# Splitting the last differential-attention head by component and moving modulation units by one tile

## What is computed

```python
sc = einsum('bqhcd,bkhcd->bhcqk', qb, k) * scale      # c: two components of 64
p = softmax(sc, axis=-1)
p = p[:, :, 0] - lam * p[:, :, 1]
o = einsum('bhqk,bkhd->bqhd', p, v)                   # v of 128 columns per head
o = rmsnorm(o, subln_g) * (1 - lambda_init)
y = (o * silu(z)) @ w_out0
```

## Time and profile before

| | us |
|---|---|
| median of 3 runs | 2986.59 |
| lowest, highest | 2982.62, 2989.71 |
| the profiled execution | 2981.39 |
| its span | 2979.5 |
| PE busy in it | 2772.0 (93%) |
| PEld busy | 2167.8 (73%) |
| DVE busy | 1681.5 (56%) |
| ACT busy | 1318.2 (44%) |

### The profile page before, as it was taken

How to read it: one execution, slowest core, us unless ns; L and a number is a source line. 1 busy time by engine, 2 the same in 40 slices (tenths; PEclk the granted TensorE clock), 3 DMA queues, 4 the chain that set the end, 5 groups by cost and what they waited for, 6 DMA issues and landing times.

```text
span 2979.5 us, 35047 instructions
## 1 busy us (share of the span) xinstructions
PE 2772.0 (93%) x13125; PEld 2167.8 (73%) x13125; DVE 1681.5 (56%) x2233; ACT 1318.2 (44%) x1881; POOL 0.2 (0%) x4
## 2 busy tenths in 40 slices
PE   6999999996899989999998899988799999999998
PEld 4777777774677767777776667666577878878787
DVE  7678888887676534344455635554764434434345
ACT  5666676664324134444343435655434323223233
POOL 0000000000000000000000000000000000000000
PEclk9999999997899999999999899999799999999999
DMA  7311111101443300000012210000211111111112
GB/s 255 104 35 50 44 34 49 49 28 56 163 134 124 113 16 16 9 6 9 6 42 98 72 40 22 22 15 15 99 36 49 44 48 48 45 49 41 52 40 84
DMA packets 216227, 168.36 MB, mean 57 GB/s; under 512 B 9578, under 2 KB 203074, under 8 KB 216130
## 3 DMA queue, kind: packets, MB, share of 16 engines
q1 hardware_dynamic: 215648, 166.88, 17.9%
q10 hardware_dynamic: 482, 0.18, 0.0%
HBM read 153.92 MB, written 13.11 MB: 56 GB/s over the span
## 4 chain that ended last, share of the span: by engine, by line
PE 79%; DVE 8%; ACT 6%; DMA 2%; DVEq 2%; issue 2%; SPq 0%; ACTq 0%
PE PS L510 18%; PE PS L512 17%; PE PS L511 17%; PE PS L1295 4%; PE PS L1957 4%; PE PS L1268 2%; PE PS L1282 2%; PE PS L1923 2%; PE PS L1272 1%; PE PS L1947 1%; PE PS L2442 1%; PE PS L2455 1%; DMA gated<-in_w_ada 1%; PE PS L2466 1%; PE PS L1915 1%
## 5 line engine op out<-in xcount | busy, mean ns | idle before, releaser
L510 PE MATMUL PS<-h_high,w_high 128*128 128x512 f32 x2096 | 845.8, 404 | 46.7 <-DVE w_low L532 18.4
L511 PE MATMUL PS<-h_low,w_high 128*128 128x512 f32 x2096 | 826.0, 394 | 0.0
L512 PE MATMUL PS<-h_high,w_low 128*128 128x512 f32 x2096 | 825.9, 394 | 0.0
L510 PEld LDWEIGHTS PS<-h_high,w_high 128*128 128x128 f32 x2096 | 399.7, 191 | 148.0 <-issue 42.5
L512 PEld LDWEIGHTS PS<-h_high,w_low 128*128 128x128 f32 x2096 | 399.0, 190 | 86.2
L511 PEld LDWEIGHTS PS<-h_low,w_high 128*128 128x128 f32 x2096 | 399.9, 191 | 80.1 <-issue 1.5
L532 DVE TENSOR_TENSOR w_low<-raw_weights,w_high 128x1024 fp32r<-128x1024 f32 (+2 forms) x156 | 179.4, 1153 | 160.3 <-ACT w_high L527 159.4
L527 ACT ACTIVATE w_high<-raw_weights 128x1024 fp32r<-128x1024 f32 (+2 forms) x156 | 155.9, 1000 | 233.7 <-PE PS L512 232.0
L1372 ACT ACTIVATE residual<-PS,rest 128x1024 f32<-128x1024 f32 x128 | 141.4, 1110 | 178.9 <-DVE rest L1502 178.9
L2998 DVE SCALAR_TENSOR_TENSOR gated<-rest,gated 128x1024 f32<-128x1024 f32 x44 | 56.6, 1286 | 254.2 <-ACT gated L2966 254.2
L849 DVE SCALAR_TENSOR_TENSOR residual<-PS,rest,residual 128x512 f32 (+1 forms) x104 | 76.4, 749 | 157.8 <-PE PS L512 153.6
(11 more groups left out here) (338 smaller groups left out, 4073.5 us busy)
## 6 DMA issues: line engine op xcount, KB each, us to landing
raw_weights<-in_w_in SPq DMA_DIRECT2D x59, 512.0 KB, 4.1
raw_weights<-in_w_up SPq DMA_DIRECT2D x44, 512.0 KB, 3.8
gated<-in_w_ada SPq DMA_DIRECT2D x12, 1536.0 KB, 7.1
raw_weights<-in_w_out SPq DMA_DIRECT2D x24, 512.0 KB, 5.0
rest<-in_ada_w SPq DMA_DIRECT2D x16, 576.0 KB, 4.9
activations<-in_ada_w SPq DMA_DIRECT2D x8, 1024.0 KB, 14.0
x_kept<-residual SPq DMA_DIRECT2D x2, 4096.0 KB, 12.5
residual<-x_kept SPq DMA_DIRECT2D x2, 4096.0 KB, 12.9
```

The lines of the kernel that those rows point to most:

```text
L510: e.matmul(out_, wh[:, k, :], xh[:, k, cols], start=first, stop=False)
L511: e.matmul(out_, wh[:, k, :], xl[:, k, cols], start=False, stop=False)
L512: return e.matmul(out_, wl[:, k, :], xh[:, k, cols], start=False, stop=last_k)
```

## The change

The last head gets its own procedures. Scores, maximum and exponential are done for each component by itself, the transposes of a block come two rounds after its scores, and the gate's products move from rounds 1 to 4 to rounds 3 to 6. The output projection has `early=7`: its first two weight tiles are split inside the head and on its end, G's first seven tiles get their high and low parts there, and TensorE multiplies them before the eighth is there. `gate_b` moves from the place of the high parts to that of the low parts. Unit 0's load waits for the last head's V transposes instead of the gating, and its products stand before the last gating. In the projection, unit u's products and matmuls come one tile later; unit 6 goes to the input projection of layer 1 with buffer `MIX_C`. Cut to its core:

```diff
-    gate_b = view(h_at, NT, HALF)
+    gate_b = view(h_at + NT * S, NT, HALF)
-    mix_stage = [view(at, NT, MCH) for at in (sc_at + 2 * S, g_at, g_at + 5 * S)]
+    mix_stage = [view(at, NT, MCH) for at in (sc_at, g_at, g_at + 5 * S)]
...
@@ OutProj.sync
             if self.units:
-                for sm, v in self.src_ready:
-                    wait(e, sm, v)
+                e.wait_ge(*self.first_unit_free)
                 mix_load(e, 0, MIX_A)
                 e.wait_ge(self.gl, self.bg + self.kt)
                 mix_load(e, 1, MIX_B)
-            with e.Fori(0, 3) as it:
+            with e.Fori(0, 2 if self.units else 3) as it:
                 for j in range(2):
                     e.wait_ge(s["ws_low"], 2 * it + (self.tile + j + 1))
                     e.dma_start(self.raw(j), self.w[:, :, bass.ds(2 * P * it + (2 + j) * P, P)]).then_inc(self.full[j], 16)
                     if self.units:
                         e.wait_ge(s["md_acc"], 2 * it + (MIX_M + 1 + j))
                         mix_load(e, 2 * it + (2 + j), (MIX_A, MIX_B)[j])
+            if self.units:
+                for j in range(2):
+                    e.wait_ge(s["ws_low"], self.tile + j + 5)
+                    e.dma_start(self.raw(j), self.w[:, :, (6 + j) * P:(7 + j) * P]).then_inc(self.full[j], 16)
+                mix_load(e, 6, MIX_C)
+                e.wait_ge(s["md_acc"], MIX_M + 6)
+                mix_load(e, 7, MIX_B)
@@ OutProj.tensor
-            if self.b == 1:
+            if self.b < 2:
                 self.rest_pe(e)
+                self.unit_pe(e, 0)
...
                 for j in range(2):
                     self.tile_pe(e, 2 * it + j, j)
-                    self.unit_pe(e, 2 * it + j)
+                    self.unit_pe(e, 2 * it + (j - 1))
             self.tile_pe(e, 6, 0)
-            self.unit_pe(e, 6)
+            self.unit_pe(e, 5)
@@ OutProj.vector
-                mix_products(e, 0, MIX_A, 32)
-                with e.Fori(0, 3) as it:
-                    for j in range(2):
-                        self.tile_dve(e, 2 * it + j, j, True)
-                        mix_out(e, 2 * it + j)
-                        mix_products(e, 2 * it + (j + 1), (MIX_B, MIX_A)[j], 16 * it + (32 + 16 * j))
+                self.tile_dve(e, 0, 0, True)
+                with e.Fori(0, 2) as it:
+                    for i in range(2):
+                        self.tile_dve(e, 2 * it + (i + 1), 1 - i, True)
+                        mix_out(e, 2 * it + i)
+                        mix_products(e, 2 * it + (i + 1), (MIX_B, MIX_A)[i], 16 * it + (32 + 16 * i))
+                self.tile_dve(e, 5, 1, True)
+                mix_out(e, 4)
+                mix_products(e, 5, MIX_B, 64)
@@ diff_attention, the last head
+        def pe_last_head(e):
+            h, prev = END, END - 1
+            for q in range(8):
+                pe_score(e, q, 0)
+                if q >= 2:
+                    pe_trans(e, h, q - 2)
+                if q == 2:
+                    pe_v(e, h)
+                pe_score(e, q, 1)
...
+                if q in (3, 5):
+                    pe_pv(e, h, (q - 3) // 2)
...
+            pe_pv(e, h, 2, False)
+            mod_pe(e, h + 3, PJ)
+            pe_trans(e, h, 6)
+            pe_trans(e, h, 7)
+            mod_pe(e, HEADS + 3, PJ, gate_b[:, 0, :], 4)
+            pe_pv(e, h, 3)
+            early_parts[0].early_pe(e, 0)
+            pe_sumsq(e, h, 1)
+            early_parts[0].early_pe(e, 1)
...
+        def dve_last_head(e):
+            h, prev, nxt = END, END - 1, early_parts[0]
+            e.sem_inc(nxt.ev, 2)
+            for q in range(8):
+                dve_max_part(e, q, 0)
+                if q:
+                    dve_probs_both(e, q - 1)
+                if q == 2:
+                    dve_v(e, h)
+                dve_max_part(e, q, 1)
+                if q == 7:
+                    dve_gate(e, h, 0)
+                    dve_probs_both(e, 7)
+                if q > 0:
+                    dve_evac(e, h, q - 1)
+                else:
+                    dve_evac(e, prev, 7)
+                if q < 3:
+                    dve_mod(e, h, q)
+                if q == 3:
+                    dve_gate(e, prev, 1)
+                if 3 <= q <= 6:
+                    dve_last_gate(e, q - 2)
+            mod_out(e, h + 3, 24 + 3 * h, column["ada_b1"] + 3 * h, PJ)
+            nxt.first_low(e, 0)
+            dve_evac(e, h, 7)
+            mod_out(e, HEADS + 3, 20, column["ada_b0"] + 20, PJ, 4)
+            for k in range(7):
+                nxt.g_low(e, k)
+                if k == 3:
+                    nxt.first_low(e, 1)
+            mix_products(e, 0, MIX_A, 32)
+            dve_gate(e, h, 1)
@@ latent_input, tensor and vector
             pe_two_tiles(e, halves, 0, pj)
+            mod_pe(e, MIX_M + 6, 4)
...
             e.memset(li_sqc, 0.0)
             e.drain()
+            mix_products(e, 6, unit_at(6), 32 + 16 * unit_count(6))
...
-    out0 = OutProj("w_out0", 0, NT, 16, True, [], [(diff["pj"], 64)], [diff["gated"]], 16, H2, units=True)
+    out0 = OutProj("w_out0", 0, NT, 16, True, [], [(diff["pj"], 64)], [diff["gated"]], 16, H2, 7, units=True)
+    out0.first_unit_free = diff["v_read"]
```

More of the change, by code:

```diff
@@ L875, in vector @@
         def vector(self, e):
-            if self.b == 0:
-                e.sem_inc(self.ev, 2)
             if self.squares:
@@ L902, in vector @@
             if self.units:
-                mix_out(e, 6)
+                mix_out(e, 5)
             if self.halves is None:
@@ L1098, in mod_out, with diff_attention @@
                         VC[:, bass.ds(bias, n)], ALU.add).then_inc(s["md_out"], 1)
-    def diff_attention():
+    def diff_attention(early_parts):
         R = Region((xt_at, NT * S), TAIL)
@@ L1283, in pe_trans, with pe_pv @@
                 last.then_inc(tr[g], 1)
-        def pe_pv(e, h, m):
+        def pe_pv(e, h, m, mod_in_bank=True):
             for g in range(2):
@@ L1291, in pe_pv @@
                 e.wait_ge(ln, 2 * h + m // 2 + 1)
-            if m == 2:
+            if m == 2 and mod_in_bank:
                 e.wait_ge(s["md_out"], h + 5)
@@ L1328, in pe_head, with part, pe_score @@
                     mod_pe(e, h + 3, MOD)
+        END = HEADS - 1
+        def part(q, c):
+            return 8 * END + 2 * q + c
+        def pe_score(e, q, c):
+            if q == 0 and c == 0:
+                e.wait_ge(qkr, END + 1)
+                e.wait_ge(kcp, 2 * END + 2)
+            e.wait_ge(ex, part(q - 1, c) + 1 if q else 8 * END)
+            own = slice(64 * c, 64 * c + 64)
+            for n in range(2):
+                e.matmul(banks(2 * c + n), QHL[c][:, q * P:(q + 1) * P], KHH[c][:, n * HALF:(n + 1) * HALF],
+                         start=True, stop=False)
+            for n in range(2):
+                last = e.matmul(banks(2 * c + n), QHL[c][own, q * P:(q + 1) * P], KL[own, n * HALF:(n + 1) * HALF],
+                                start=False, stop=True)
+            last.then_inc(sc, 1)
+        def pe_last_head(e):
[7 more added lines that the diff above has]
+                pe_score(e, q, 1)
+                if q == 0:
+                    pe_trans(e, prev, 7)
+                if q == 1:
+                    pe_pv(e, prev, 3)
+                if q == 2:
+                    pe_sumsq(e, prev, 1)
+                if q in (3, 5):
+                    pe_pv(e, h, (q - 3) // 2)
+                if q == 6:
+                    pe_sumsq(e, h, 0)
+            pe_pv(e, h, 2, False)
[7 more added lines that the diff above has]
+            early_parts[0].early_pe(e, 1)
         def tensor(e):
@@ L1334, in tensor @@
                 pe_head(e, it, it - 1, it + 1)
[L1335 to L1339, removed]
+            pe_last_head(e)
         def act_chunk(e, hh, c):
@@ L1451, in act_head, with act_exp_part, act_last_head @@
                     act_query_high(e, nxt, QUERIES)
+        def act_exp_part(e, q, c):
+            i = 2 * (q % 2) + c
+            e.wait_ge(mx, part(q, c) + 1)
+            e.activation(E1 if c else E0[q % 2], banks(2 * c, 2), ACT.Exp, bias=negmax[:, i:i + 1], scale=SCALE,
+                         accum_out=rowsum[:, i:i + 1]).then_inc(ex, 1)
+        def act_last_head(e):
+            h, prev, nxt = END, END - 1, early_parts[0]
+            for q in range(8):
+                act_exp_part(e, q, 0)
+                if q == 2:
+                    act_v(e, h)
+                act_exp_part(e, q, 1)
+                if q > 0:
+                    act_evac(e, h, q - 1)
+                else:
+                    act_evac(e, prev, 7)
+                if q == 1:
+                    act_o(e, prev, 1)
+                if q == 2:
+                    act_rstd(e, prev, 1)
+                if q in (3, 4):
+                    nxt.first_high(e, q - 3)
+                if q == 5:
+                    act_o(e, h, 0)
+                if q == 6:
+                    act_rstd(e, h, 0)
+            for k in range(3):
+                nxt.g_high(e, k)
```

(52 more changed lines are left out.)

## The result

The changed kernel takes 3003.14 us (median of 5 runs, 2996.83 to 3005.27), the kernel before, run beside it, 2985.26 (5 runs, 2982.62 to 2989.71). The ratio is 1.006, 95% interval 1.0044 to 1.0077: slower by 17.9 us.

The account below looks back on a forecast made before the run. It took TensorE's idle time before 787.9 us as what can be won, the output projection being full. Terms -12.5 + 18.8 + 5.2 = +11.5 us on the median 2986.6 gave 2998 us, range 2984 to 3008.

Parts of the forecast that it names:

- case A: Whole kernel: head gain, exposed projection loads and later unit 6 sum to +11.5 us; own range +5 to +18, chance 0.60.
- Part 1: Last differential head, worked out by component on VectorE: last transposes at 749.6 us against 764.77 before.
- The waits on the transposes: Last head: transposes stand behind scores and value products in TensorE's order; nothing to 3.8 us each, 3.0 in all.
- Rival C: Last head stays with TensorE: value products delay transposes each time, last ones at 756 or later; 3005 to 3011, chance 0.12.
- Part 2: Last transposes to the end of the projection input's last low part: 25.8 us, ending at 775.4, 12.5 us sooner.
- G': End of the last low part of the output projection's input, when SP issues unit 1's load; predicted at 775.4 us.
- Part 3: Output projection with units one tile later: tile loads exposed behind unit loads, 108.6 us against 89.8, +18.8 (14 to 22).
- P1: Output projection: end of VectorE's products for unit 1, predicted 24.4 us after G'.
- three rounds: Output projection, tiles 4, 5 and 6: exposed loads make rounds of 18.3, 17.7 and 17.7 us, 53.7 together, against 11.84 each.
- the tail: Output projection, tiles 6 and 7 after the last round: 30.5 us, with unit 7's load ahead of the next projection's weights.
- Rival B: Projection rounds: weight tile not held behind the unit's load, rounds of 13.9 or 13.4 us; net -7.3, 2979.3; chance 0.11.
- Part 4: Latent projection: TensorE waits for unit 6 in front of tile 2; +5.2 us (3.5 to 6.5).

## Why the prediction was right

It gave 2998.0 us, 2984 to 3008, slower with 0.72; measured were 3003.1. The case that it took, A, is what happened, and the experiments show its mechanism. The size is less good than the time looks: the +11.5 us were put on 2986.6, the median of three runs, where the five runs have 2985.3, so that the time was missed by 5.1 us and the change, +17.9, by 6.4. It lies at the very end of case A's own range of +5 to +18. Against its steps:

**Part 1 (last transposes at T' = 749.6): 751.92, 2.3 us late.** A maximum over 1024 columns takes 1.22 us, just what the line through the two neighbouring sizes gave. The wait for the gate weights is gone. The waits on the transposes were under-sized: 3.0 us were taken for all, and 6.3 came, 4.3 of them in one place, where the first value product of this head (16 matmuls, 6.25 us at 706.06) stands ahead of the transposes. The bound of 3.8 us for one such wait used 5.4 us for that product; it took 6.25. Rival C had such waits each time and T' at 756 or later; one of them came at full length, and the last transposes came at 751.9.

```profile
683.13 1.22 DVE L1669 TENSOR_REDUCE rest<-PS 128x1 f32<-128x1024 f32 x1
...
714.06 0.69 DVE L1601 COPY rest<-PS 128x512 f32<-128x512 f32 x1 [4.30 <-PE PS L1290]
```

**Part 2 (T' to G', 25.8): 27.0.** All of the 1.2 us is unit 0's load: it landed 17.65 us after T', where 16.4 were worked out. VectorE waited 7.4 us for it, at the place that the text named. Parts 1 and 2 together brought 9.0 us and not 12.5: 12.85 by the head, of which 3.8 are lost again, since this stretch was 23.2 long before. What the prediction did not ask is whether the new place of unit 0 costs something by itself; it does, since with unit 0 ahead of the fetch, all else of the stretch alike, unit 1's load goes out at T'+23.8.

**Part 3 (108.6 us from G' to the end of tile 7): 110.2.** P1 at G'+25.6 for 24.4, three rounds in 55.0 for 53.7, the tail 29.6 for 30.5. P1 is late mostly because tile 2's load landed in 8.66 us, where 7.68 stood; a round was right to 0.4 us on average. Half of the 1.3 us for the three rounds is addition: the prediction's own terms for a round, 0.2, 1.1 or 0.6, 7.7, 2.34, 1.8 and 5.3, give 18.4 and 17.9 us and not 18.3 and 17.7, so 54.3 for three. Rival B, the tile load that isn't held up by the unit's, is out by the same rows. Two signs were off: TensorE was busy 80% from 800 to 855 (clock 0.88), not 60 to 70%, and the projection ended at 889.1, not near 884. The first was at odds with the prediction's own 13.8 us of TensorE in a round of 18, which is 77%.

**The clock.** TensorE after 8.2 us of idle at 791 ran at 0.54 for 6 us, half speed, as expected. And it fell after each shorter wait too. The rows are the 6 us behind the first wait and 6.5 to 7 us behind each of the three waits of the rounds:

```profile
791.00:797.00 6.00, 5.79 (x15) 4.56 (x16) 3.36 (x5) 2.00 (x2) 0.00 (x0) 0.54 0.25 77
...
823.00:830.00 7.00, 6.86 (x25) 5.76 (x26) 1.50 (x3) 1.06 (x1) 0.00 (x0) 0.70 0.84 262
...
841.00:848.00 7.00, 6.91 (x20) 5.71 (x21) 1.35 (x3) 1.06 (x1) 0.00 (x0) 0.52 0.77 259
...
859.50:866.00 6.50, 6.45 (x21) 5.37 (x22) 4.21 (x6) 2.00 (x2) 0.00 (x0) 0.59 0.01 3
```

As the text had it, the next load covers the first two and the third is paid. The rule of the Trainium skill, page TensorE: Matmul & The Clock Gate (HAM oscillation), that a loop which waits for its DMA starts each group at the low clock, is borne out by these rows; in steps of 1 us TensorE begins at a granted clock of 0.50 behind each of the four waits.

**Part 4 (+5.2): +5.7 in the trace, 5.0 by the run that moves the order.** The 2.2 us that the rest of the latent projection adds were not foreseen; its last rounds, in which SP issues one unit's load after the other, are 12.5 to 13.5 us long where they were 12.3 to 12.6. The new head alone, which leaves the units where they were, has one such round of 13.8 us in each of its two traces, so that the late units need not be the cause; no run here separates it.

**The sum** was +11.5 us; the trace has 17.2 for the same terms, and 19.4 with the 2.2. The 5.7 us of miss are T' (2.3: the waits 3.3 longer, other terms 1.0 shorter), unit 0's landing (1.2), the projection (1.6) and unit 6 (0.6).

## What to carry to other kernels

A queue of loads is a list of promises: when work moves behind another step, look at what its buffer's release was letting through, and how long before its use each load behind it in the queue is issued. Here moving eight short vector instructions by one tile turned a load issued a whole round of 12 us ahead of need into one issued at need. With the unit that was left over for the next stage, the move cost 27 us by itself. In the whole change, each tile's load a unit earlier gave back 19 us, and the last unit's load behind the next stage's tiles another 7.5. Price a reordering by its rounds first: three rounds of 18 against 12 were readable from the rows of the old profile.

## What the runs showed that was not expected

**A shorter wait did not cost less clock.** After 6.72 us of idle the 7 us from 823 had a granted clock of 0.70, after 4.15 us the 7 us from 841 had 0.52, and after 3.52 us the 6.5 us from 859.5 had 0.59. With 1.2 and 2.4 GHz as the only levels, TensorE was at the lower one for some 4.2, 6.7 and 5.3 us. Waits of 3.5 to 4 us thus cost more here than one of 6.7, on top of the wait itself. In steps of 1 us the profile shows where the difference lies: the clock had fallen 2.7 us before TensorE started again in the first, 0.2 in the second and 1.6 in the third, and what lies in the wait costs nothing more. Why it fell when it did, no run here shows.

**A load behind a long one landed a little later than its bytes say.** Unit 0's 1.5 MB behind the 4 MB fetch took 17.23 us from its issue; by bytes, from the fetch's 12.8 and 0.43 MB/us, 16.3 after the fetch's issue were worked out, and it was 17.65.
